# Attention and retention steps placed one piece earlier beside the input projection

## The chip, the cores and the metric

One core of one Trainium2 chip runs the whole kernel. The metric is the device time of the kernel in microseconds (us), the median of several runs.

## The reference

One encoder layer on 256 frames of width 2048, all in float32:

```python
h = rms_norm(x, norm1_g)
proj = h @ w_in                 # 2048 x 7168: retention q,k,v,gate and attention q,k,v
ret = silu(rg) * head_group_norm(retention(rotary(rq), rotary(rk), rv))        # 8 heads of 128
att = chunk_attention(rms_norm(aq), rms_norm(ak), av, rel_bias)                # 8 heads of 128
x = x + concatenate([ret, att]) @ w_out
x = x + square(relu(rms_norm(x) @ w_ff1)) @ w_ff2                              # width 8192
```

Retention multiplies the scores of a head with a decay mask that is causal over chunks of 64 frames; attention is a softmax over the scores plus a bias.

## The kernel before

**Products in three passes.** Each float32 matrix is split into a high part and a rest. For every piece of weights ScalarE writes the high part (`w_hi`, `in_hi`, L993), VectorE subtracts it from the raw weights (`w_lo`, `in_lo`, L1403), and TensorE runs three passes: high by high (L739), low input by high weight (L746), high input by low weight (L752). The last pass alone needs `w_lo`.

**The input stage.** The projection is done in four blocks of two heads each (i = 0 to 3; attention heads 2i and 2i + 1, retention heads u = 2i and 2i + 1). A block walks through 19 slabs, each of two pieces, so 38 pieces with positions 0 to 37:

```python
STEPS = "I0 I1 I2 I3 J0 Q1 J1 P5 J2 P6 J3 P7 P3 Z1 Q2 Z2 P4 H1 H2".split()
```

I and J are the two attention heads (384 columns); the others are the retention columns of both heads (512 columns), where seven products (Q1, P5, P6, P7, P3, Q2, P4) stand for eight, after Strassen and Winograd. So the first half of Q1 is position 10, J1 is 12 and 13, P5 is 14 and 15, P6 is 18 and 19, J3 20 and 21, P7 22 and 23, Z1 26 and 27, P4 32 and 33, H1 34 and 35, H2 36 and 37. P5 and P6 need sums of raw slabs, made by VectorE (`in_sum`, L1412); P7 and P4 need a further slab that a GpSimd DMA adds. `set_y` and `set_h` (ScalarE) and `set_z` and `set_w` (VectorE) move the common products between banks; the second tile of Z1 waits for `set_w`. For block 0 alone VectorE also builds the combinations of the input (`s_first`, L1431, four additions; `s_second`, `s_third`, `s_lo`), and ScalarE their high parts (`s_hi`).

**Attention and retention run beside it.** Each step of a head is a function on one engine: TensorE transposes q and k (`att_T`), ScalarE and VectorE scale them (`att_qT`, `att_kT`), TensorE makes the scores, VectorE adds the bias and takes the maximum, ScalarE takes the exponential, VectorE normalises (`att_probs`), TensorE transposes (`att_PT`) and multiplies with v (`att_pv`), and `att_mix` on ScalarE and then on VectorE splits the result. Ahead of them `att_squares` (ScalarE), `att_mean_squares` (VectorE, writes `a_ms`), a power on GpSimd (`a_rs`, L534) and `att_norm` (VectorE, writes `a_qk`) normalise q and k. Retention is alike: `ret_proj` (ScalarE), `ret_rotate` and `ret_rotated` (VectorE, the latter writes `r_qk`), `ret_T`, `ret_qT`, `ret_kT`, `ret_scores`, `ret_decay`, `ret_y`, `ret_norm`, a power on GpSimd (`r_rs`, L538), `ret_scale`, `ret_ZT`, `ret_mix`.

**What sets the order.** Nothing is scheduled at run time. Each engine has a list written by hand: `at_piece(i, pos, f, h)` puts step f at piece pos of block i. The loops are

```python
for q in range(8 * G_OUT):        # TensorE
    in_piece(q)
    for f in work.get(q, ()): f()
for q in range(8 * G_OUT):        # ScalarE with in_hi, VectorE with in_lo
    in_hi(q + 2)
    for f in work.get(q, ()): f()
```

so TensorE runs a step right after its piece, and ScalarE and VectorE run it after the split of the piece two further on. Steps of one position run in the order in which they were listed. An engine works strictly in its order and waits on semaphores, so a step that is late holds up all that stands behind it. `in_hi(q)` waits until piece q - 4 is used up. The loads of raw slabs (SyncE's queue) wait for `in_lo` of the slab that had the buffer.

After the input stage the output projection (from `G_OUT` on) and the two feed-forward products run; the change doesn't touch them.

Of the kernel before, what the change touches and what calls it, by code (L numbers as in the profile page):

```python
# [39 lines left out]
PIECES = 8  # L40
# [34 lines left out]
def hybrid_block(nc, x, x_cols, w_att, w_ret, w_out, w_up, w_down, gains, rel_windows, rope_cos, rope_sin, decay, out):  # L75
# [3 lines left out]
    with ExitStack() as ctx:  # L79
# [501 lines left out]
        def _(pe):  # L581
# [185 lines left out]
            def at_piece(i, pos, f, *args):  # L767
                work.setdefault(IN_PIECES * i + pos, []).append(lambda: f(*args))

            for i in range(BLOCKS):  # L770
                for h, places in ((2 * i, (13, 15, 19, 21)), (2 * i + 1, (27, 28, 31, 33))):
                    for pos, f in zip(places, (att_T, att_scores, att_PT, att_pv)):
                        at_piece(i, pos, f, h)
                at_piece(i, 35, ret_T, 2 * i)
                at_piece(i, 36, ret_scores, 2 * i)
                at_piece(i, 37, ret_y, 2 * i)
                at_piece(i + 1, 1, ret_ZT, 2 * i)
# [187 lines left out]
        def _(act):  # L965
# [174 lines left out]
            for f, pos in enumerate((9, 10, 13, 14)):  # L1140
                at_piece(0, pos, s_hi, f)
            for i in range(BLOCKS):
# [4 lines left out]
                at_piece(i, 13, att_qT, h)  # L1147
                at_piece(i, 16, keep_in_p5, i)
                at_piece(i, 17, att_exp, h)
                at_piece(i, 19, att_pT, h)  # L1150
                at_piece(i, 21, att_mix, h)
                at_piece(i, 22, att_proj, h + 1)
                at_piece(i, 23, set_y, i)
                at_piece(i, 24, att_squares, h + 1)
                at_piece(i, 25, set_h, i)
                at_piece(i, 27, att_qT, h + 1)
                at_piece(i, 29, att_exp, h + 1)
                at_piece(i, 31, att_pT, h + 1)
                at_piece(i, 32, ret_proj, u)
                at_piece(i, 33, att_mix, h + 1)  # L1160
                at_piece(i, 34, ret_exp, u)
                at_piece(i, 35, ret_qT, u)
                at_piece(i + 1, 0, ret_scale, u)
                at_piece(i + 1, 0, ret_proj, u + 1)
                at_piece(i + 1, 1, ret_mix, u)
# [231 lines left out]
        def _(dve):  # L1397
# [225 lines left out]
            at_piece(0, PIECES - 1, s_first)  # L1623
            at_piece(0, 8, s_second)
            at_piece(0, 10, s_lo, 0)
            at_piece(0, 12, s_third)
            at_piece(0, 13, s_lo, 1)
            at_piece(0, 16, s_lo, 2)
            at_piece(0, 17, s_lo, 3)
            for i in range(BLOCKS):  # L1630
                h, u, late = 2 * i, 2 * i, i == BLOCKS - 1
                at_piece(i, 10, att_mean_squares, h)
                at_piece(i, 11, att_norm, h)
                at_piece(i, 11, in_sum, i, "b", "Q1")
                at_piece(i, 13, att_kT, h)
# [327 lines left out]
```

## Time and profile before

| | |
|---|---|
| median of 3 runs | 1124.0 us (1123.88 to 1124.03) |
| the profiled execution | 1123.88 us, its span 1122.1 us |
| TensorE matmul busy | 1104.2 us, 98% of the span |
| VectorE busy | 884.6 us, 79% |
| ScalarE busy | 688.3 us, 61% |
| GpSimd busy | 54.2 us, 5% |
| mean granted TensorE clock | 0.998 of full speed |

The profile is of one execution; its span runs from the first to the last instruction, and 1.78 us of its time lie around the span. Busy time is what an engine spent in instructions. The trace also tells for each idle stretch which instruction of another engine ended it. A block of the input stage takes 86.4 us (Z1 of block 0 starts at 67.07 us, that of block 1 at 153.47 us).

### The profile page before, as it was taken

Reading aid. Unit: us, or ns where it says so; the run is one execution under the profiler, and the core shown is the slowest. Engines: PE = TensorE matmul, PEld = TensorE weight load, DVE = VectorE, ACT = ScalarE, POOL = GpSimd, SP = SyncE. Lnnn points to the kernel's source line nnn. Section 1 sums busy time; section 2 is a strip of 40 time slices with the busy share of each in tenths; the row PEclk is TensorE's granted clock in tenths of the full one; section 3 lists DMA queues with packets and bytes.
Section 4 is the critical chain, followed back from the end, with each engine's and each line's share of the span. In section 5 each row is a group of like instructions: output and inputs, shape, how many; then the busy total and the mean of one; then the engine's idle time right before and its main releaser. Section 6 shows DMA issues by size and latency. Waiting matters only on the chain.

```text
span 1122.1 us, 13185 instructions
## 1 busy us (share of the span) xinstructions
PE 1104.2 (98%) x5198; PEld 933.7 (83%) x5198; DVE 884.6 (79%) x881; ACT 688.3 (61%) x809; POOL 54.2 (5%) x66
## 2 busy tenths in 40 slices
PE   9799999999999999999999999999999999999998
PEld 9688888988988888888888888888888888888887
DVE  6878777777787768878788778788779788779784
ACT  6565565574565446668756568655667755577652
POOL 0100100100100000000000000000000000000000
PEclk9999999999999999999999999999999999999999
DMA  9785584585576556796797797797787797787792
GB/s 363 261 248 182 156 271 161 166 264 174 169 241 262 187 225 188 230 294 218 233 284 241 249 275 228 230 292 230 262 263 229 247 273 236 257 280 218 246 276 95
DMA packets 42958, 263.81 MB, mean 235 GB/s; under 512 B 4752, under 2 KB 6544, under 8 KB 15120
## 3 DMA queue, kind: packets, MB, share of 16 engines
q1 hardware_dynamic: 36704, 220.22, 52.6%
q0 software_dynamic: 5760, 41.95, 20.3%
q8 instruction: 41, 0.67, 0.2%
q10 hardware_dynamic: 432, 0.81, 0.2%
q14 instruction: 21, 0.17, 0.0%
HBM read 260.85 MB, written 2.10 MB: 234 GB/s over the span
## 4 chain that ended last, share of the span: by engine, by line
PE 85%; DVE 7%; ACT 3%; issue 2%; POOL 1%; ACTq 0%; DVEq 0%
PE acc L869 10%; PE acc L867 10%; PE acc L871 10%; PE acc L739 5%; PE acc L746 5%; PE acc L752 5%; PE bankC L829 4%; PE bankC L824 4%; PE acc L824 4%; PE acc L822 4%; PE bankC L822 4%; PE acc L829 4%; DVE w_lo L1403 3%; PE acc L591 2%; PE acc L596 2%
## 5 line engine op out<-in xcount | busy, mean ns | idle before, releaser
L1690 DVE TENSOR_TENSOR w_lo<-raw,w_hi 128x2048 fp32r<-128x2048 f32 x180 | 410.9, 2288 | 126.9 <-ACT w_hi L1206 126.7
L1206 ACT ACTIVATE w_hi<-raw 128x2048 fp32r<-128x2048 f32 x180 | 344.7, 1916 | 219.5 <-PE acc L871 145.5
L1403 DVE TENSOR_TENSOR w_lo<-raw,w_hi 128x1024 fp32r<-128x1024 f32 (+1 forms) x152 | 167.5, 1106 | 52.4 <-ACT w_hi L993 52.3
L993 ACT ACTIVATE w_hi<-raw 128x1024 fp32r<-128x1024 f32 (+1 forms) x152 | 143.1, 963 | 40.9 <-DVE raw L1412 32.5
L739 PE MATMUL acc<-w_hi,hT_hi 128*128 128x384 f32 (+1 forms) x416 | 105.5, 372 | 0.3 <-ACT w_hi L993 0.2
L867 PE MATMUL acc<-w_hi,hF_hi 128*128 128x512 f32 x256 | 100.8, 394 | 0.0
L871 PE MATMUL acc<-w_hi,hF_lo 128*128 128x512 f32 x256 | 99.7, 390 | 0.0
L869 PE MATMUL acc<-w_lo,hF_hi 128*128 128x512 f32 x256 | 99.7, 389 | 0.0
L746 PE MATMUL acc<-w_hi,hT_lo 128*128 128x384 f32 (+1 forms) x416 | 99.2, 356 | 0.0
L752 PE MATMUL acc<-w_lo,hT_hi 128*128 128x384 f32 (+1 forms) x416 | 98.9, 356 | 0.0
L867 PE MATMUL acc<-w_hi,dF_hi 128*128 128x512 f32 x248 | 96.9, 391 | 0.0
L871 PE MATMUL acc<-w_hi,dF_lo 128*128 128x512 f32 x248 | 96.5, 389 | 0.0
L869 PE MATMUL acc<-w_lo,dF_hi 128*128 128x512 f32 x248 | 96.5, 389 | 0.0
L746 PEld LDWEIGHTS acc<-w_hi,hT_lo 128*128 128x128 f32 x416 | 75.6, 188 | 7.0
L752 PEld LDWEIGHTS acc<-w_lo,hT_hi 128*128 128x128 f32 x416 | 75.4, 188 | 6.5
L739 PEld LDWEIGHTS acc<-w_hi,hT_hi 128*128 128x128 f32 x416 | 72.8, 188 | 6.5 <-ACT w_hi L993 1.0
L1698 DVE TENSOR_TENSOR raw<-raw 128x2048 f32<-128x2048 f32 x32 | 73.1, 2285 | 0.0
L871 PEld LDWEIGHTS acc<-w_hi,hF_lo 128*128 128x128 f32 x256 | 48.0, 188 | 10.1
L867 PEld LDWEIGHTS acc<-w_hi,hF_hi 128*128 128x128 f32 x256 | 48.1, 188 | 9.9
L869 PEld LDWEIGHTS acc<-w_lo,hF_hi 128*128 128x128 f32 x256 | 48.1, 188 | 9.4
L871 PEld LDWEIGHTS acc<-w_hi,dF_lo 128*128 128x128 f32 x248 | 46.6, 188 | 9.7
L867 PEld LDWEIGHTS acc<-w_hi,dF_hi 128*128 128x128 f32 x248 | 46.6, 188 | 9.6
(262 smaller groups left out, 1813.8 us busy)
## 6 DMA issues: line engine op xcount, KB each, us to landing
raw<-in_w_up SPq DMA_DIRECT2D x64, 1024.0 KB, 6.2
raw<-in_w_down SPq DMA_DIRECT2D x64, 1024.0 KB, 6.1
raw<-in_w_ret SPq DMA_DIRECT2D x32, 1024.0 KB, 5.3
raw<-in_w_att SPq DMA_DIRECT2D x28, 768.0 KB, 4.2
raw<-in_w_out SPq DMA_DIRECT2D x16, 1024.0 KB, 4.9
raw<-in_w_up POOLq DMA_DIRECT2D x16, 1024.0 KB, 8.9
raw<-in_w_down POOLq DMA_DIRECT2D x16, 1024.0 KB, 8.6
raw<-in_w_ret POOLq DMA_DIRECT2D x8, 1024.0 KB, 8.5
```

The costliest lines, as they stand in the source:

```text
L739: nc.tensor.matmul(bank[:, 0:wide], stationary(step, m, t)[0], piece(w_hi, q, start, start + wide), start=fresh, stop=False, skip_group_ch ...
L746: nc.tensor.matmul(bank[:, 0:n], stationary(step, m, t)[1], piece(w_hi, q, start, start + n), start=False, stop=False, skip_group_check=True)
L752: mm = nc.tensor.matmul(bank[:, 0:n], stationary(step, m, t)[0], piece(w_lo, q, start, start + n), start=False, stop=t == SLAB_KT - 1, ski ...
L822: nc.tensor.matmul(bank[:], hi[:, form, tile_cols(t)], wh[:, cols], start=first and t == 0, stop=False, skip_group_check=True)
L824: nc.tensor.matmul(bank[:], lo[:, form, tile_cols(t)], wh[:, cols], start=False, stop=False, skip_group_check=True)
L867: nc.tensor.matmul(banks[m][:], hi[:, form + m, tile_cols(t)], wh[:, cols], start=False, stop=False, skip_group_check=True)
L869: nc.tensor.matmul(banks[m][:], hi[:, form + m, tile_cols(t)], wl[:, cols], start=False, stop=False, skip_group_check=True)
L871: mm = nc.tensor.matmul(banks[m][:], lo[:, form + m, tile_cols(t)], wh[:, cols], start=False, stop=t == SLAB_KT - 1, skip_group_check=True)
L993: nc.scalar.activation(piece(w_hi, q, 0, n), raw[:, r, half * n:(half + 1) * n], ACT.Copy).then_inc(hi_done, 1)
L1206: nc.scalar.activation(w_hi[:, ring(s)], raw[:, r, :], ACT.Copy).then_inc(slab_hi, 1)
L1403: nc.vector.tensor_tensor(piece(w_lo, q, 0, n), raw[:, IN_PLAN[i, READ_AT.get(step, step)][0], half * n:(half + 1) * n], piece(w_hi, q, 0, ...
L1690: nc.vector.tensor_tensor(w_lo[:, ring(s)], raw[:, r, :], w_hi[:, ring(s)].bitcast(f32), ALU.subtract).then_inc(slab_lo, 1)
```

## The change

Only positions in the three lists change; no instruction is added or removed. Most steps of attention and the retention steps of the first head of a block move one piece earlier on all three engines. Some go otherwise: on VectorE `s_first` moves from position 7 to 8 and `s_third` from 12 to 9; `in_sum` of P5 moves ahead of `in_lo` of the piece 13 and of `att_norm`; `ret_rotate` stays at 33 and `ret_rotated` at 34; `set_w` goes from 23 to 24 and the second head's `att_mean_squares` stays at 24, now behind it. On ScalarE the second head's `att_squares` and `set_y` change places. GpSimd's and SyncE's programs are the same.

```diff
@@ TensorE
-                for h, places in ((2 * i, (13, 15, 19, 21)), (2 * i + 1, (27, 28, 31, 33))):
-                    for pos, f in zip(places, (att_T, att_scores, att_PT, att_pv)):
-                        at_piece(i, pos, f, h)
-                at_piece(i, 35, ret_T, 2 * i)
-                at_piece(i, 36, ret_scores, 2 * i)
-                at_piece(i, 37, ret_y, 2 * i)
-                at_piece(i + 1, 1, ret_ZT, 2 * i)
+                for h, first in ((2 * i, 12), (2 * i + 1, 26)):
+                    at_piece(i, first, att_T, h)
+                    at_piece(i, (14, 27)[h % 2], att_scores, h)
+                    at_piece(i, (18, 30)[h % 2], att_PT, h)
+                    at_piece(i, (20, 32)[h % 2], att_pv, h)
+                at_piece(i, 34, ret_T, 2 * i)
+                at_piece(i, 35, ret_scores, 2 * i)
+                at_piece(i, 36, ret_y, 2 * i)
+                at_piece(i + 1, 0, ret_ZT, 2 * i)
@@ ScalarE
-            for f, pos in enumerate((9, 10, 13, 14)):
+            for f, pos in enumerate((9, 10, 12, 13)):
                 at_piece(0, pos, s_hi, f)
...
-                at_piece(i, 13, att_qT, h)
+                at_piece(i, 12, att_qT, h)
                 at_piece(i, 16, keep_in_p5, i)
-                at_piece(i, 17, att_exp, h)
-                at_piece(i, 19, att_pT, h)
-                at_piece(i, 21, att_mix, h)
+                at_piece(i, 16, att_exp, h)
+                at_piece(i, 18, att_pT, h)
+                at_piece(i, 20, att_mix, h)
                 at_piece(i, 22, att_proj, h + 1)
-                at_piece(i, 23, set_y, i)
-                at_piece(i, 24, att_squares, h + 1)
+                at_piece(i, 23, att_squares, h + 1)
+                at_piece(i, 24, set_y, i)
                 at_piece(i, 25, set_h, i)
-                at_piece(i, 27, att_qT, h + 1)
-                at_piece(i, 29, att_exp, h + 1)
-                at_piece(i, 31, att_pT, h + 1)
+                at_piece(i, 26, att_qT, h + 1)
+                at_piece(i, 28, att_exp, h + 1)
+                at_piece(i, 30, att_pT, h + 1)
                 at_piece(i, 32, ret_proj, u)
-                at_piece(i, 33, att_mix, h + 1)
-                at_piece(i, 34, ret_exp, u)
-                at_piece(i, 35, ret_qT, u)
-                at_piece(i + 1, 0, ret_scale, u)
+                at_piece(i, 32, att_mix, h + 1)
+                at_piece(i, 33, ret_exp, u)
+                at_piece(i, 34, ret_qT, u)
+                at_piece(i, 37, ret_scale, u)
                 at_piece(i + 1, 0, ret_proj, u + 1)
-                at_piece(i + 1, 1, ret_mix, u)
+                at_piece(i + 1, 0, ret_mix, u)
@@ VectorE
-            at_piece(0, PIECES - 1, s_first)
+            at_piece(0, 8, s_first)
             at_piece(0, 8, s_second)
+            at_piece(0, 9, s_third)
             at_piece(0, 10, s_lo, 0)
-            at_piece(0, 12, s_third)
-            at_piece(0, 13, s_lo, 1)
-            at_piece(0, 16, s_lo, 2)
-            at_piece(0, 17, s_lo, 3)
+            at_piece(0, 11, s_lo, 1)
+            at_piece(0, 13, s_lo, 2)
+            at_piece(0, 15, s_lo, 3)
...
                 at_piece(i, 10, att_mean_squares, h)
+                at_piece(i, 10, in_sum, i, "b", "Q1")
                 at_piece(i, 11, att_norm, h)
-                at_piece(i, 11, in_sum, i, "b", "Q1")
-                at_piece(i, 13, att_kT, h)
+                at_piece(i, 12, att_kT, h)
                 at_piece(i, 14, in_sum, i, "d", "P5")
-                at_piece(i, 15, att_bias_max, h)
-                at_piece(i, 18, att_probs, h)
+                at_piece(i, 14, att_bias_max, h)
+                at_piece(i, 17, att_probs, h)
                 at_piece(i, 20, set_z, i)
-                at_piece(i, 21, att_mix, h)
-                at_piece(i, 23, set_w, i)
+                at_piece(i, 20, att_mix, h)
+                at_piece(i, 24, set_w, i)
                 at_piece(i, 24, att_mean_squares, h + 1)
-                at_piece(i, 26, att_norm, h + 1)
-                at_piece(i, 27, att_kT, h + 1)
-                at_piece(i, 28, att_bias_max, h + 1)
-                at_piece(i, 30, att_probs, h + 1)
+                at_piece(i, 25, att_norm, h + 1)
+                at_piece(i, 26, att_kT, h + 1)
+                at_piece(i, 27, att_bias_max, h + 1)
+                at_piece(i, 29, att_probs, h + 1)
+                at_piece(i, 32, att_mix, h + 1)
                 at_piece(i, 33, ret_rotate, u)
-                at_piece(i, 33, att_mix, h + 1)
                 at_piece(i, 34, ret_rotated, u)
-                at_piece(i, 35, ret_kT, u)
+                at_piece(i, 34, ret_kT, u)
                 at_piece(i, 35, ret_sigmoid, u)
-                at_piece(i, 36, ret_decay, u)
-                at_piece(i, 37, ret_norm, u)
+                at_piece(i, 35, ret_decay, u)
+                at_piece(i, 36, ret_norm, u)
...
-                at_piece(i + 1, 1, ret_mix, u)
+                at_piece(i + 1, 0, ret_mix, u)
```

## Rows read from the trace of the kernel before

**Rows 1.** The page, engines: busy us, share of the span, instructions.

```profile
PE 1104.2 (98%) x5198; PEld 933.7 (83%) x5198; DVE 884.6 (79%) x881; ACT 688.3 (61%) x809; POOL 54.2 (5%) x66
```

**Rows 2.** Windows: one block, all after the input stage; stretch, length, busy, clock, DMA.

```profile
104.00:190.00 86.00, 83.86 (x434) 73.93 (x433) 66.77 (x113) 49.09 (x91) 5.86 (x6) 1.00 0.63 200
440.00:1122.00 682.00, 679.26 (x3076) 564.03 (x3075) 546.20 (x344) 436.46 (x374) 27.51 (x32) 1.00 0.78 245
```

**Rows 3.** What TensorE waited for, 20 to 366 us: total us, times, longest.

```profile
PE bankD L739 <- ACT w_hi L993: 4.4, 4, 2.6
PE bankB L639 <- DVE a_p L1512: 3.0, 4, 1.4
PE bankC L752 <- DVE w_lo L1403: 2.9, 6, 0.8
PE bankA L652 <- DVE r_qk L1538: 2.6, 4, 0.9
```

**Rows 4.** Timeline of block 0: start us, us, instruction, in brackets idle before.

```profile
26.83 2.50 DVE L1431 TENSOR_TENSOR s_blk<-hT_hi,hT_lo 128x512 f32<-128x512 f32 x4
27.71 1.06 ACT L993 ACTIVATE w_hi<-raw 128x1024 fp32r<-128x1024 f32 x1 [1.75 <-DMA raw<-in_w_ret]
...
33.11 0.73 PE L752 MATMUL bankC<-w_lo,hT_hi 128*128 128x512 f32 x2 [0.79 <-DVE w_lo L1403]
...
41.48 1.22 PE L739 MATMUL bankD<-w_hi,sf_hi 128*128 128x512 f32 x2 [2.63 <-ACT w_hi L993]
...
56.39 0.55 PE L639 MATMUL bankB<-ident,a_p 128*128 128x128 f32 x3 [1.40 <-DVE a_p L1512]
```

**Rows 5.** Windows: the stretch just after block 0's longest wait.

```profile
41.50:44.80 3.30, 3.30 (x8) 2.63 (x9) 3.30 (x4) 2.78 (x5) 0.21 (x1) 0.50 0.74 117
```

**Rows 6.** Timeline of block 1, positions 11 to 19.

```profile
124.52 0.95 DVE L1403 TENSOR_TENSOR w_lo<-raw,w_hi 128x768 fp32r<-128x768 f32 x1
124.69 1.64 POOL L534 TENSOR_TENSOR a_rs<-a_ms,neg_half 128x4 f32<-128x4 f32 x1 [8.60 <-DVE a_ms L1479]
...
127.16 2.29 DVE L1412 TENSOR_TENSOR raw<-raw 128x2048 f32<-128x2048 f32 x1
...
129.40 0.38 PE L624 MATMUL bankA<-ident,a_qk 128*128 128x128 f32 x2
...
142.79 0.55 PE L639 MATMUL bankB<-ident,a_p 128*128 128x128 f32 x3 [0.53 <-DVE a_p L1512]
```

**Rows 7.** Timeline of GpSimd's powers, 20 to 160 us.

```profile
27.07 1.02 POOL L527 TENSOR_TENSOR rstd<-me,neg_half 128x2 f32<-128x2 f32 x1 [25.57 <-DVE me L1614]
...
115.39 0.70 POOL L538 TENSOR_TENSOR r_rs<-r_ve,neg_half 128x2 f32<-128x2 f32 x1 [14.72 <-DVE r_ve L1569]
...
154.57 1.03 POOL L534 TENSOR_TENSOR a_rs<-a_ms,neg_half 128x4 f32<-128x4 f32 x1 [12.20 <-DVE a_ms L1479]
```

**Rows 8.** Timeline of block 1, `set_y` and `set_w`.

```profile
151.29 0.61 ACT L1089 ACTIVATE acc<-bankC 128x512 f32<-128x512 f32 x1
...
152.59 0.69 DVE L1425 TENSOR_TENSOR acc<-in_p,bankC 128x512 f32<-128x512 f32 x1
```

**Rows 9.** Timeline of block 1, from the end of `att_pv` to `ret_T`.

```profile
171.74 0.38 PE L645 MATMUL bankA<-a_pT,a_proj 128*128 128x128 f32 x2
...
172.18 0.39 ACT L1045 ACTIVATE zT_hi<-bankA 128x256 fp32r<-128x256 f32 x1
172.32 1.22 DVE L1403 TENSOR_TENSOR w_lo<-raw,w_hi 128x1024 fp32r<-128x1024 f32 x1 [0.87 <-ACT w_hi L993]
...
174.94 0.42 DVE L1517 TENSOR_TENSOR zT_lo<-bankA,zT_hi 128x256 fp32r<-128x256 f32 x1
...
176.41 0.69 DVE L1538 TENSOR_TENSOR r_qk<-r_c,r_s 128x512 f32<-128x512 f32 x1
...
177.44 0.38 PE L652 MATMUL bankC<-ident,r_qk 128*128 128x128 f32 x2
```

**Rows 10.** Timeline of block 1, `ret_T` of the second head of block 0.

```profile
107.73 0.44 PE L652 MATMUL bankA<-ident,r_qk 128*128 128x128 f32 x2 [0.58 <-DVE r_qk L1538]
```

## The prediction

> **What bounds the kernel now.** I read the page first: TensorE is busy for 98% of the span [rows 1]. The windows by stage say where the rest is: 682 us after the input stage hold under 3 us of idle TensorE, while one block of the input stage holds 2.1 us in 86 us [rows 2]. So the change can only act on TensorE's waits in the four blocks. The waits of that stretch sum to 12.9 us in 18 waits [rows 3]: four of `ret_T` for `r_qk`, which belong to the second heads, and the others around P5, P6 and `att_PT`. The timeline then shows the order of events. Block 0 has the worst: 0.79 us in Q1, 2.63 us before P5, 1.40 us before `att_PT` [rows 4]. After the 2.63 us of idleness the granted clock is 0.50, the level of 1.2 GHz, for 3.4 us [rows 5], and P5 pays about 1.7 us; after 1.40 us it stays at 1.00. The stage is balanced so finely that a position moved by one piece (1.4 us for half of P4, P5 or P6, 2.1 us for J, 2.7 us for Z and H) matters only by what waits for it.
>
> I follow the new lists by hand with the old durations. A split of 1024 columns takes 1.06 us on ScalarE [rows 4] and 1.22 us on VectorE [rows 9], and the next instruction begins 0.08 us before the end; one of 768 takes 0.95 us on VectorE and gives way after 0.87 [rows 6].
>
> **Block 0, its head.** `s_first` (2.50 us [rows 4]) ran while VectorE had to wait anyway: piece 10's high part ends at 28.77 because its load is late [rows 4]. At position 8 it runs behind `in_lo` of piece 10, so VectorE idles 1.9 us and then does 28.79 + 1.14 + 2.53 (`s_first`) + 1.33 (`s_second`) = 33.79 before `in_lo` of piece 11. Q1's last pass starts at about 35.05 in place of 33.11 [rows 4]. From there VectorE itself is the chain, with everything ahead of `att_PT` on it: splits, `s_third` 1.20, two `in_sum` of 2.20, three `s_lo` of 0.60, `att_norm` 0.79, `att_kT` 0.40, `att_bias_max` 1.38, `att_probs` 0.74, and one wait of 0.7 for piece 15. It sums to `a_p` at 55.05, against 56.33. `att_T` in the meantime waits until 42.3 and TensorE is idle 3 to 4 us. `att_PT` starts 1.3 us sooner, but one half of P6 (1.37 us) now stands behind it: the head of block 0 comes out at 0.0 us, up to +0.4 if P5 and J1 run at the low clock again.
>
> **Blocks 1 to 3, their head.** `in_sum` (2.29 us) may start where piece 13's split started, at 124.52, in place of 127.16 [rows 6]. That makes P5's high part early, and pushes `in_lo` of 13 and `att_norm` behind it: 124.52 + 2.20 + 0.87 + 0.11 (for `a_rs`, below) + 0.87 = 128.57. TensorE ends the first half of J1 at 127.32 and wants `att_T` there; it ran at 129.40 before [rows 6]. New wait 1.3 us, where the waits in P5 (1.2 us with the restarts) go. On along VectorE: splits of 14 to 19, `in_sum`, `att_kT`, `att_bias_max` and `att_probs`, with 0.8 us of waiting for high parts, give `a_p` at 140.34, against 142.7 before; `att_PT` starts 2.4 us earlier than 142.79 [rows 6], less 1.37 for the half of P6 that is now behind it: gain 1.0 us in each of three blocks, 3.0 in all. Bounds: 0 if the order on VectorE stretches by another 1.0, and 1.5 if `a_p` is ready when TensorE asks.
>
> **Z1, every block.** Counted from the start of P7, `set_y` ran at 3.38 and `set_w` at 4.68 (P7 at 147.91) [rows 8]. With `att_squares` (1.17) ahead of it on ScalarE, `set_y` goes to 4.7 at its end and `set_w` to 6.17 at its end, behind `in_lo` of piece 26. Z1's second tile asks at 5.95: 0.27 us and a restart, 0.35 (bounds 0 and 0.6). Then `att_mean_squares` comes at 6.1 with `in_lo` of 27 right behind it. GpSimd's power `a_rs` takes 1.03 us beside an idle VectorE [rows 7] and 1.64 us when it starts inside a split [rows 6], ending 0.86 us after that split's end. So it ends at 7.37 + 0.86 = 8.23, `a_qk` at 9.14, and `att_T`, wanted at 8.58, waits 0.62 and a restart: 0.70 (bounds 0, if `a_rs` takes 1.03, and 1.0). Sum 1.05 us, four times 4.2.
>
> The case that most divides these sums is that power. The rows say: 1.64 within a split; and a power of two columns takes 1.02 us, begun amid four additions back to back, against 0.70 us alone [rows 7], so it gets in when one instruction ends and need not wait for the last. That gives the 0.11 us above. The Trainium skill, page "SBUF — State Buffer", section "Who interferes with whom", has the rule: a VectorE instruction with two inputs in SBUF and a GpSimd instruction that reads SBUF share one read port, and the second blocks until the first ends. By that rule, the trace agrees; a power that overlaps freely would take 1.03 everywhere and the total below would be 2.8 lower.
>
> **`ret_T` of the first head, every block.** This is the largest term. `ret_T` moves from behind H1's second half to behind its first, 2.72 us. What feeds it is moved less. `att_pv` ends at 172.12; ScalarE then splits `zT_hi`, then the high part of a piece, and VectorE from the low part of that piece (172.32) to the end of `r_qk` (177.10) needs 4.78 us, 0.34 of it the rest of `att_mix` [rows 9]. Now `in_hi` of piece 35 stands behind `att_mix`, and VectorE's `in_lo` of 35 behind that, with `ret_rotate` and `ret_rotated` still at 33 and 34. From the end of `att_pv`: 0.06 + 0.26 + 1.06 + 0.02 + 4.44 = 5.84 us. TensorE, from the same point, has the second half of P4 (1.46) and the first of H1 (2.72), less 0.24 by which the next piece overlaps the end: 3.94. Before, both halves of H1 lay there and 0.3 us was to spare [rows 9]. So TensorE waits 1.9 us, with restart 2.0, and four times 8.0. Each duration is a row's, and both sides hang on TensorE's own `att_pv`, so I hold it to 1.7 to 2.2 a block. The steps behind it (`ret_decay`, `ret_norm`, `ret_scale`, `ret_ZT`) have over 0.5 us to spare each; loads and the GpSimd DMAs are asked for no later relative to their use.
>
> **`ret_T` of the second head.** It waited 0.58 us, with restart and pipeline end 0.83 [rows 10], three times, and 1.2 in the last block (0.9 in [rows 3]). `ret_ZT` and `ret_mix` of the first head now run one piece earlier, and `r_qk` comes 1 us before it is asked for. Gain 3.7 us; below, 0.
>
> **Sum.** 0.0 - 3.0 + 4.2 + 8.0 - 3.7 = +5.5 us, against the profiled execution's own 1123.88: 1129.4; that execution lies 0.1 under the median, so 1129.4 stands for either. Outside the input stage nothing moves.
>
> **The rivals.** (B) GpSimd isn't held and `set_w` is in time: 4.2 falls away, +1.3, 1125.3, no measurable change. The two lengths of `a_rs` speak against it, the small slack of `set_w` for it. 22%. (C) Faster: ScalarE and VectorE reach `r_qk` before the new `ret_T`. It decides at 1.9 us less than the 5.84 of that chain, and would take the 8.0 away: -2.5, 1121.4. Also here: the early moves bring what the waits before P5, P6 and `att_PT` suggest. [Rows 9] speak against it. 11%. (D) GpSimd is kept out until VectorE truly idles: in the head the power then ends one split later, 1.0 us a block, +4.0, 1133.3. The 1.02 us row speaks against it. 8%. (E) The clock falls to the 1.2 GHz level after each new `ret_T` wait, as it did after 2.63 us, and takes 1.7 us each: +6.8, 1136.1. The idle time there is some 1.7 us by the profile's count, nearer the 1.40 that left the clock alone. 7%. The Trainium skill, page "TensorE: Matmul & The Clock Gate", section "HAM oscillation — how this bites in real kernels", tells that a wait that recurs in a loop can bring the low clock back each time; by it the time would be E's. The forecast has 52%, its own range 1127.0 to 1131.5.
>
> **How the numbers follow.** The range takes in B and most of D: 1123.8 to 1133.0; C and E are left out. About 0.2% (2.2 us) is what a measurement tells from no change. Slower by more: forecast, D and E, less 3% for a small forecast, 0.64. The same: B and that edge, 0.25. Faster: C, 0.11.
>
> **What would show it.** Right: `ret_T` on banks C and D waits for `r_qk` some 1.7 us four times, and no longer on bank A; `att_T` waits for `a_qk` over 1 us; the wait of L739 on bank D is gone; `a_rs` takes some 3 us at the heads. Wrong: no wait at `ret_T` of the first heads (C), a clock of 0.50 after them (E), `a_rs` of 1.03 in the second heads (B), or block 0's head more than 1 us off.

## The result, and the profile after

The changed kernel takes 1133.4 us (median of four runs, 1133.2 to 1134.0); beside it the kernel before took 1123.9 us (1123.8 to 1124.0). The ratio is 1.0085, 95% interval 1.0067 to 1.0102: slower by 9.4 us. The forecast was 1129.4 with a range up to 1133.0, so the direction was right and the size was not. The profiled execution of the changed kernel took 1134.24 us, 10.36 more than that of before. One of the six runs of experiment 11 took 6357 us and is left out of the range given there.

The page of the changed kernel, engines:

```profile
PE 1105.7 (98%) x5198; PEld 935.2 (83%) x5198; DVE 887.1 (78%) x881; ACT 690.2 (61%) x809; POOL 64.3 (6%) x66
```

Against [rows 1] TensorE, VectorE and ScalarE do the same work in 1.5 to 2.5 us more; GpSimd alone is busy 10 us longer, with the same 66 instructions. The page's view says nothing more: 10 us of lost time hide behind a rounded 98%.

One block, from Z1 to the next Z1, and work after the input stage, by windows (stretch, length, then busy time of TensorE's matmuls and weight loads, VectorE, ScalarE and GpSimd, granted clock, DMA):

```profile
69.60:157.80 88.20, 84.45 (x435) 74.36 (x434) 67.75 (x113) 49.97 (x91) 8.05 (x6) 1.00 0.62 195
337.00:1120.00 783.00, 780.74 (x3542) 647.50 (x3541) 626.11 (x453) 494.15 (x449) 29.95 (x36) 1.00 0.76 242
```

The second stretch has 2.3 us of idle TensorE in 783, as little as in [rows 2]; the block has grown from 86.4 to 88.2 us, and 3.75 us of it are idle against 2.1. So the loss is in the input stage, where the changed lists are.

What TensorE waited for in the changed kernel (total us, times, longest):

```profile
PE bankA L624 <- DVE a_qk L1488: 9.0, 8, 3.9
PE bankC L652 <- DVE r_qk L1540: 7.2, 4, 1.8
PE bankC L752 <- DVE w_lo L1405: 3.2, 1, 3.2
...
PE acc L739 <- DVE acc L1427: 0.8, 4, 0.2
```

(Line numbers of ScalarE and VectorE are two higher than before; two waits of 1.6 us, which lie before 20 us, are left out.) The waits of P5 for `w_hi`, of `att_PT` for `a_p` and of the second head's `ret_T` on bank A [rows 3] are gone. In their place stand eight of `att_T`, four of the first heads' `ret_T` on bank C, four for `set_w`, and one of 3.2 us in block 0. The change exchanged waits, and the new ones are longer.

**Block 0** is the first place to look. Its timeline (start, length, instruction, in brackets the idle time before it and what ended it):

```profile
35.33 1.22 PE L752 MATMUL bankC<-w_lo,hT_hi 128*128 128x512 f32 x2 [3.17 <-DVE w_lo L1405]
...
43.53 0.69 PE L624 MATMUL bankA<-ident,a_qk 128*128 128x128 f32 x2 [3.85 <-DVE a_qk L1488]
```

and what VectorE and GpSimd did ahead of the second wait, from their timelines:

```profile
37.94 2.28 DVE L1414 TENSOR_TENSOR raw<-raw 128x2048 f32<-128x2048 f32 x1
40.14 0.95 DVE L1405 TENSOR_TENSOR w_lo<-raw,w_hi 128x768 fp32r<-128x768 f32 x1
41.01 0.68 DVE L1451 TENSOR_TENSOR sf_lo<-s_mix,sf_hi 128x512 fp32r<-128x512 f32 x1
42.60 0.87 DVE L1488 TENSOR_SCALAR a_qk<-a_proj,a_rs 128x128 f32<-128x128 f32 x4 [0.91 <-POOL a_rs L534]
```

```profile
38.11 4.46 POOL L534 TENSOR_TENSOR a_rs<-a_ms,neg_half 128x4 f32<-128x4 f32 x1 [2.74 <-DVE a_ms L1481]
```

The power on four columns took 4.46 us. It began in `in_sum`, lasted through the split and `s_lo`, and ended at 42.57, 0.88 after the last of the three. `att_norm` stood behind it, and VectorE was idle 0.91 us. What became of that at `att_PT`, with one more wait of VectorE on the way:

```profile
46.13 1.23 DVE L1405 TENSOR_TENSOR w_lo<-raw,w_hi 128x1024 fp32r<-128x1024 f32 x1 [0.97 <-ACT w_hi L995]
...
56.46 0.35 DVE L1514 TENSOR_SCALAR a_p<-a_e,a_rc 128x256 f32<-128x256 f32 x1
...
57.58 0.49 PE L639 MATMUL bankB<-ident,a_p 128*128 128x128 f32 x3
```

`a_p` ends at 56.81, and TensorE asks for it at 57.58. The clock is in the windows:

```profile
35.00:39.00 4.00, 3.67 (x12) 3.41 (x13) 4.00 (x7) 2.29 (x6) 1.26 (x2) 0.57 1.05 387
39.00:43.00 4.00, 0.67 (x4) 0.35 (x3) 3.09 (x6) 2.06 (x3) 4.00 (x2) 0.89 0.27 77
43.00:50.00 7.00, 6.47 (x23) 6.17 (x24) 5.96 (x9) 3.52 (x5) 0.58 (x1) 0.58 1.00 221
50.00:54.00 4.00, 4.00 (x23) 3.69 (x22) 3.93 (x9) 2.85 (x7) 0.00 (x0) 1.00 0.09 18
```

The clock fell to the 1.2 GHz level with each of the two waits; before it fell once [rows 5]. A mean of 0.57 over 4 us is 0.50 for 3.4 us; the next two rows give another 0.9 and 5.9 us in the same way, 10.2 us in all against 3.3 in [rows 5]. Against the same pieces of block 1, the end of Q1 and the first half of J1 took 1.6 us more, and `att_T` with the second half of J1 and the first half of P5 2.5 us more. The first 1.6 us cost nothing: TensorE was done at 39.68 and then stood still for 3.85 us until `a_qk` came. The starts of the pieces give the balance: J3 begins 2.61 us later than before. The two waits are 7.0 us; before there were five, of 0.62, 0.79, 2.63, 0.37 and 1.40, together 5.8 us, each with its restart (the first products after a wait take longer: `att_T`'s two took 0.44 us in block 1 of the changed kernel and 0.38 in that of before). In the last row TensorE is busy without a gap, and it stays so through P6: `a_p` is ready when P6's half ends.

**Blocks 1 to 3, their heads.** The piece starts show J3 0.84 us earlier against Q1 in each block, and 0.89 up to Z1 (forecast 1.0). The timeline of block 1 has the power of 2.98 us that the prediction worked out, and the wait of `att_T` that it said:

```profile
129.96 2.98 POOL L534 TENSOR_TENSOR a_rs<-a_ms,neg_half 128x4 f32<-128x4 f32 x1 [8.61 <-DVE a_ms L1481]
...
133.92 0.44 PE L624 MATMUL bankA<-ident,a_qk 128*128 128x128 f32 x2 [1.18 <-DVE a_qk L1488]
```

**Z1 to H1** costs 1.54 us a block (forecast 1.05). Block 1's timeline, TensorE and GpSimd:

```profile
158.67 0.73 PE L739 MATMUL acc<-w_hi,hT_hi 128*128 128x512 f32 x2 [0.21 <-DVE acc L1427]
158.77 1.93 POOL L534 TENSOR_TENSOR a_rs<-a_ms,neg_half 128x4 f32<-128x4 f32 x1 [12.58 <-DVE a_ms L1481]
...
161.67 0.44 PE L624 MATMUL bankA<-ident,a_qk 128*128 128x128 f32 x2 [0.41 <-DVE a_qk L1488]
...
170.86 0.35 DVE L1514 TENSOR_SCALAR a_p<-a_e,a_rc 128x256 f32<-128x256 f32 x1
...
171.26 0.55 PE L639 MATMUL bankB<-ident,a_p 128*128 128x128 f32 x3
```

The wait for `set_w` with its restart costs about 0.45 us and that of `att_T` about 0.55. The last two rows are one that no list of waits names: `a_p` ends at 171.21 and `att_PT` begins at 171.26. Before, `a_p` ended 0.7 us ahead of it. The transpose is not shown as waiting since the modelled end of the piece ahead covers the gap, but the piece starts grow by 0.4 us there.

**`ret_T` of the first heads.** Both sides, as worked out, in block 1 (VectorE's chain, then TensorE):

```profile
177.01 0.42 DVE L1519 TENSOR_TENSOR zT_lo<-bankA,zT_hi 128x256 fp32r<-128x256 f32 x1 [1.33 <-ACT zT_hi L1047]
177.96 1.23 DVE L1405 TENSOR_TENSOR w_lo<-raw,w_hi 128x1024 fp32r<-128x1024 f32 x1 [0.52 <-ACT w_hi L995]
...
180.58 1.22 DVE L1405 TENSOR_TENSOR w_lo<-raw,w_hi 128x1024 fp32r<-128x1024 f32 x1
181.72 0.68 DVE L1540 TENSOR_TENSOR r_qk<-r_c,r_s 128x512 f32<-128x512 f32 x1
```

```profile
182.46 0.44 PE L652 MATMUL bankC<-ident,r_qk 128*128 128x128 f32 x2 [1.79 <-DVE r_qk L1540]
```

VectorE is idle 1.33 us until `att_pv` and ScalarE's split are done, 0.52 more for the next high part, and only then come `ret_rotate`, a split and `ret_rotated`. It is idle with work in hand: the rotation needs nothing of `att_pv`.

### The profile page after: what moved, and what is told of

Same layout as the page of the kernel before. It is cut to its first block, busy times and chain, and to the rows that moved or that the text cites. A ratio compares the mean times of both kernels' runs of the same rounds, so it can differ in the third digit from the quotient of the medians.

```text
span 1132.4 us, 13184 instructions
## 1 busy us (share of the span) xinstructions
PE 1105.7 (98%) x5198; PEld 935.2 (83%) x5198; DVE 887.1 (78%) x881; ACT 690.2 (61%) x809; POOL 64.3 (6%) x66
## 4 chain that ended last, share of the span: by engine, by line
PE 82%; DVE 6%; ACT 5%; issue 3%; POOL 2%; DMA 2%; ACTq 0%; DVEq 0%
PE acc L873 10%; PE acc L871 10%; PE acc L869 10%; PE bankC L831 4%; PE acc L831 4%; PE bankC L826 4%; PE acc L826 4%; PE acc L824 4%; PE bankC L824 4%; PE acc L739 4%; PE acc L746 4%; PE acc L752 4%; ACT w_hi L995 3%; DVE w_lo L1405 2%; PE acc L591 2%
## 5 line engine op out<-in xcount | busy, mean ns | idle before, releaser
L739 PEld LDWEIGHTS acc<-w_hi,hT_hi 128*128 128x128 f32 x416 | 73.4, 191 | 10.2 <-DVE acc L1427 2.5
```

The source lines that it names most:

```text
L739: nc.tensor.matmul(bank[:, 0:wide], stationary(step, m, t)[0], piece(w_hi, q, start, start + wide), start=fresh, stop=False, skip_group_ch ...
```

## The experiments

Times are medians; the kernel before ran beside each set, at 1123.91, 1123.96, 1124.05 and 1124.08 us. Where a block is named, differences come from the starts of its pieces.

### 1. The changed kernel once more

> The changed kernel as it is. If the longer time of block 0's head comes from the order of the lists, GpSimd's first power a_rs is again 4.4 to 4.5 us long, the clock is again low for about 10 us in all around 36 to 49 us, and the time is 1133.4 within 0.7. If it came from chance (the phase of a clock window or a late load in that one execution), the first power or the low stretches differ and the time moves by up to 2 us.

1133.7 us (1133.4 to 1133.9), ratio 1.0086 (1.0071 to 1.0101). Every power of the input stage came back at the same length, 4.46 us too, and every wait but one, so they follow from the lists. The one is `att_T`'s in block 0, 3.15 us in place of 3.85, and the clock has changed beside it:

```profile
39.00:43.00 4.00, 1.29 (x5) 0.78 (x3) 3.09 (x6) 2.06 (x3) 4.00 (x2) 0.50 0.26 61
...
46.00:50.00 4.00, 4.00 (x18) 3.73 (x17) 3.96 (x4) 2.11 (x4) 0.00 (x0) 0.73 0.97 199
```

These are windows of its block 0. Here the clock stays low from the wait in Q1 on, through the idle time ahead of `att_T`, where the other execution had it back for a while, and it rises about 0.8 us sooner behind. TensorE takes longer for J1 and waits that much less: `att_T` starts at 43.43 against 43.53. Behind it `att_PT` starts at 57.16 against 57.58, and J3 is 2.2 us late in place of 2.6. So the low clock in the head is no accident of one execution, but its borders move; ahead of `att_T` it costs nothing, behind `att_T` it does.

### 2. `s_first` back at position 7

```diff
-            at_piece(0, 8, s_first)
+            at_piece(0, PIECES - 1, s_first)
```

> The changed kernel with s_first back at position 7, in VectorE's idle time. Theory (VectorE's order sets block 0's head): Q1's last pass comes 2 us earlier, att_T about 2.2 us earlier, and the head and the whole kernel gain about 2.0 us, 1131.4. Rival (GpSimd's held power or the low clock sets it alone): att_T moves by less than 0.5 us or the low clock takes the gain back, and the kernel stays at 1133.4 within 0.5.

1131.4 us (1131.3 to 1131.6), ratio 1.0066 (1.0049 to 1.0083): 2.4 us back against experiment 1, the changed kernel in the same set. The wait in Q1 is 0.8 us again, and the low clock behind it is gone; behind `att_T` it is low for one stretch of 3.4 us, as long as before. The waits:

```profile
PE bankA L624 <- DVE a_qk L1488: 10.3, 8, 5.1
...
PE bankC L752 <- DVE w_lo L1405: 1.4, 2, 0.8
```

All of block 0's loss goes (J3 at -0.3 against before), although `att_T` now waits 5.1 us and the power is still 4.46 us long. So the four additions in the wrong gap are what this kernel loses in block 0. Their way there is VectorE's own chain: `a_qk` begins 2.1 us sooner (40.48 against 42.60) and `a_p` ends 2.1 to 2.2 us sooner (54.59 against 56.71 in experiment 1 and 56.81). That leaves at most 0.3 us of the 2.5 at J3 against experiment 1 for the clock.

### 3. `s_lo(1)` of block 0 behind `att_norm`

```diff
-            at_piece(0, 11, s_lo, 1)
...
                 at_piece(i, 11, att_norm, h)
+                if i == 0:
+                    at_piece(0, 11, s_lo, 1)
```

> The changed kernel with one VectorE step of block 0, s_lo of the second combination, moved from ahead of att_norm to behind it. Theory (GpSimd's power is held while VectorE goes from one instruction with two inputs in SBUF straight to the next, and got in early in blocks 1 to 3 because att_norm had to wait there): the first a_rs falls from 4.46 us to 2.98 as in the other blocks, or to 3.8 if it has to let the split of piece 13 pass, and att_T of block 0 starts 0.9 to 1.5 us earlier. The kernel gains 0.5 to 1.5 us, for the low clock takes part of it. Rival (something else of block 0 holds the power, such as the DMA traffic of the first 40 us): it stays at 4.46 and att_T where it was.

1132.9 us (1132.7 to 1133.3), ratio 1.0080 (1.0066 to 1.0093), 0.8 less than the changed kernel run again. The first power is shorter by the 0.60 us of the instruction that no longer stands between:

```profile
38.23 3.86 POOL L534 TENSOR_TENSOR a_rs<-a_ms,neg_half 128x4 f32<-128x4 f32 x1 [2.76 <-DVE a_ms L1481]
...
128.35 2.98 POOL L534 TENSOR_TENSOR a_rs<-a_ms,neg_half 128x4 f32<-128x4 f32 x1 [8.61 <-DVE a_ms L1481]
```

In block 0 it ends 0.88 us after piece 13's split, in block 1 0.87 us after the end of `in_sum`, one instruction sooner, and the order on VectorE is the same in both: `in_sum`, split, `att_norm`. So VectorE's back-to-back instructions hold the power in block 0, and something that differs between the blocks decides whether it gets in after one of them. These runs don't show what. `att_T` starts 0.4 to 0.5 us sooner (43.05), less than the 0.9 expected. And the clock is not the same: it is low from 34.3 to 41.1 us and back at 1.00 when `att_T` starts. TensorE then comes to `att_PT` first and waits 1.07 us for `a_p`, which ends at 55.88, and J3 is 1.0 us late. So with the clock up it is VectorE's chain that sets block 0's head, and the 0.8 us hold some of the clock.

### 4. `ret_rotate` ahead of `att_mix`, one position earlier

```diff
+                at_piece(i, 32, ret_rotate, u)
                 at_piece(i, 32, att_mix, h + 1)
-                at_piece(i, 33, ret_rotate, u)
-                at_piece(i, 34, ret_rotated, u)
+                at_piece(i, 33, ret_rotated, u)
```

> The changed kernel with ret_rotate of the first head at 32, ahead of att_mix on VectorE, and ret_rotated at 33, behind one split less. Theory (ret_T waits for what VectorE does behind att_mix): the rotation falls into VectorE's wait for att_mix, r_qk comes 1.5 to 2 us earlier, the four waits of ret_T on bank C of 1.8 us go, and the kernel gains 7.5 to 8.0 us: 1125.6. Rival (the wait is only passed on to ret_scores or ret_y, whose chain is also tight): it gains under 3 us, and new waits stand at ret_scores, ret_y or ret_ZT.

1125.8 us (1125.4 to 1126.4, ten runs), ratio 1.0017 (1.0008 to 1.0026): 7.9 us back, the whole term. The waits are those of the changed kernel (the longest of `att_T` 3.8 in place of 3.9) without the row of L652:

```profile
PE bankA L624 <- DVE a_qk L1488: 9.0, 8, 3.8
PE bankC L752 <- DVE w_lo L1405: 3.2, 1, 3.2
```

### 5. The second head's mean squares ahead of `set_w`

```diff
-                at_piece(i, 24, set_w, i)
                 at_piece(i, 24, att_mean_squares, h + 1)
+                at_piece(i, 24, set_w, i)
```

> The changed kernel with the second head's att_mean_squares ahead of set_w, so that GpSimd's power starts beside set_w, which has one input in PSUM, and not inside a split with two inputs in SBUF. Theory (two SBUF inputs hold GpSimd's read): the four powers of 1.93 us become 1.03, a_qk comes 0.9 us earlier, att_T's wait of 0.41 goes, gain 0.5 to 0.7 us in each block, 2.0 to 2.8 in all: 1131.0. Rival (any VectorE instruction beside it slows the power): it stays at 1.7 or more and the time at 1133.4 within 0.7.

1132.0 us (1130.9 to 1132.1), ratio 1.0069 (1.0054 to 1.0084): 1.7 us back, less than expected: `set_w` itself is now a little later, and the loss at `att_PT` stays. The mechanism shows in block 1's timeline:

```profile
157.46 0.69 DVE L1427 TENSOR_TENSOR acc<-in_p,bankC 128x512 f32<-128x512 f32 x1
...
157.64 1.03 POOL L534 TENSOR_TENSOR a_rs<-a_ms,neg_half 128x4 f32<-128x4 f32 x1 [11.98 <-DVE a_ms L1481]
158.06 1.22 DVE L1405 TENSOR_TENSOR w_lo<-raw,w_hi 128x1024 fp32r<-128x1024 f32 x1
...
158.20 0.74 PE L739 MATMUL acc<-w_hi,hT_hi 128*128 128x512 f32 x2 [0.28 <-DVE acc L1427]
```

Begun beside `set_w`, which reads one operand from PSUM, the power takes 1.03 us, as begun beside an idle VectorE [rows 7], and a split that starts later doesn't hold it. The second heads' `att_T` no longer waits. Rival B's price for the power (1.03 us) is thus what another order gives; in the changed kernel it was 1.93 us.

### 6. All three together

> The three edits to the changed kernel at once: s_first at 7, ret_rotate ahead of att_mix at 32 with ret_rotated at 33, att_mean_squares ahead of set_w. Theory (they take away separate waits): the gains add, 2.2 + 7.8 + 1.7 = 11.7 us off 1133.5, so 1121.8, which is faster than before. Rival (they cover each other, or a wait removed late in a block returns in the next head): 1124 or more.

1121.5 us (1121.2 to 1122.3, eleven runs), ratio 0.9979 (0.9970 to 0.9987). The three parts add up: 2.4 + 7.9 + 1.7 is 12.0, and 12.2 came back. With them the changed lists are faster than those before, by 2.4 us.

The head of block 0 has the same order on every engine as in experiment 2, and its profiled execution prices the clock. `att_T` starts at 41.41 in experiment 2 and at 41.47 here; behind it the clock is low for 3.4 us there and for 6.1 here. `att_PT`, first there and then here:

```profile
54.65 0.55 PE L639 MATMUL bankB<-ident,a_p 128*128 128x128 f32 x3
```

```profile
55.85 0.49 PE L639 MATMUL bankB<-ident,a_p 128*128 128x128 f32 x3
```

That is 1.2 us for one longer low stretch, and 1.2 at J3 too (-0.3 and +0.9). `a_p` itself ends at 54.59 and 55.03, so up to 0.4 us of it comes through VectorE's chain. The eleven runs spread over 1.1 us.

### 7. The first head's `att_T` at 13 again

```diff
-                for h, first in ((2 * i, 12), (2 * i + 1, 26)):
+                for h, first in ((2 * i, 13), (2 * i + 1, 26)):
...
-                at_piece(i, 12, att_qT, h)
+                at_piece(i, 13, att_qT, h)
...
-                at_piece(i, 12, att_kT, h)
+                at_piece(i, 13, att_kT, h)
```

> The changed kernel with the first head's att_T, att_qT and att_kT back at position 13 and all else as changed. Theory (att_T at 12 asks 1.3 us too early and stops TensorE, while att_PT is set by VectorE's order): the wait of 1.2 us goes in all blocks, block 0 idles 2.5 us in place of 3.9, and blocks 1 to 3 gain about 0.7 us each at J3; in all 2.1 to 4 us: 1130.5. Rival (the early att_T pays for itself by an earlier a_p): no gain or a loss, 1133.5 to 1135.

1130.4 us (1130.2 to 1130.5), ratio 1.0057 (1.0041 to 1.0072), 3.4 us better than the changed kernel run again, as expected. TensorE does half of J1 in place of waiting:

```profile
PE bankB L639 <- DVE a_p L1514: 2.6, 4, 0.9
PE bankA L624 <- DVE a_qk L1488: 2.2, 5, 0.6
```

`att_PT` waits instead, 0.9 us at most, and `att_scores` of block 0 once, 1.3 us, but that costs less than the 1.2 to 3.9 us at the first heads' `att_T`. About half of the gain, 1.6 us at J3, is block 0's, where the clock is also low for 6.8 us in place of 13.7.

### 8. The kernel before with the retention part alone

```diff
-                at_piece(i, 35, ret_T, 2 * i)
-                at_piece(i, 36, ret_scores, 2 * i)
+                at_piece(i, 34, ret_T, 2 * i)
+                at_piece(i, 35, ret_scores, 2 * i)
...
-                at_piece(i, 34, ret_exp, u)
+                at_piece(i, 33, ret_exp, u)
```

and likewise `ret_y`, `ret_ZT`, `ret_qT`, `ret_kT`, `ret_decay`, `ret_norm`, `ret_scale` and `ret_mix`; `ret_rotate` and `ret_rotated` stay.

> The kernel before with the retention part of the change alone: ret_T, ret_scores, ret_y, ret_ZT of the first head and what belongs to them on ScalarE and VectorE one piece earlier, attention untouched. Theory (ret_T of the first head cannot be moved without its rotation): r_qk ends at 177.1 as before while TensorE asks at 174.7, a wait of 2.4 us and restart, four times 2.5 lost, 3.7 gained at the second head's ret_T: +6.3, 1130.2. Rival (the loss comes only together with att_pv's move, since the rotation hangs on it): under 2 us lost, 1126 or less.

1132.2 us (1131.8 to 1132.4), ratio 1.0072 (1.0058 to 1.0086): 8.2 us slower than before, where 6.3 was expected. Blocks 0 and 2 lose 1.75 us each on balance, and block 1 3.4. The timeline and a window there say why:

```profile
178.70 0.66 PE L652 MATMUL bankC<-ident,r_qk 128*128 128x128 f32 x2 [2.28 <-DVE r_qk L1538]
...
179.44 2.06 PE L739 MATMUL acc<-w_hi,hT_hi 128*128 128x512 f32 x4
```

```profile
179.10:182.50 3.40, 3.40 (x12) 2.77 (x11) 1.74 (x3) 2.06 (x3) 0.00 (x0) 0.55 0.02 5
```

The four products of the pass take 2.06 us where they take 1.17 at full clock: the 1.2 GHz level after one wait of 2.28 us. The other three waits of that length left the clock at 1.00. This is the event of rival E, once in four and worth 1.65 us. Where the wait is 1.79 us, as in the changed kernel, it never came: 24 waits in the six profiled executions that have it.

### 9. The same with `ret_rotate` at 32 and `ret_rotated` at 33

> The kernel before with the retention part of the change, and ret_rotate at 32 and ret_rotated at 33. Theory (the rotation's place is the whole cause of the loss with the retention part): no wait at the first heads' ret_T, none at the second heads', so 3.5 us under the kernel before: 1120.4. Rival (ret_T at 34 passes its wait on to a later step): 1123 or more.

1121.2 us (1120.9 to 1121.6, eight runs), ratio 0.9975 (0.9965 to 0.9985). The rotation stands ahead of `att_mix`. The waits of the input stage are those of [rows 3] with the same numbers, less the last row, that of `ret_T`, and with one of 0.2 us more. So the second head's gain is real, and all but a little of the first head's cost was in the rotation's place. By the piece starts the second heads give the 3.7 us of the changed kernel, and the first heads still cost 0.3 us a block, which they don't in experiment 6 (`ret_T` of block 1 begins 0.06 us after the end of `r_qk` here, at 174.12, and 0.73 after it there); that is why 2.8 us came of the 3.5 expected.

### 10. `att_norm` ahead of `in_sum`

All three edits of experiment 6, and

```diff
-                at_piece(i, 10, att_mean_squares, h)
+                at_piece(i, 9, att_mean_squares, h)
+                at_piece(i, 10, att_norm, h)
                 at_piece(i, 10, in_sum, i, "b", "Q1")
-                at_piece(i, 11, att_norm, h)
```

with `s_third` at 11 and the third `s_lo` at 15 in block 0.

> The kernel with all three edits, and its head ordered anew on VectorE: att_mean_squares of the first head at 9, where VectorE has 0.7 us free, att_norm at 10 ahead of in_sum, s_third at 11 and the third s_lo at 15. Theory (the power inside in_sum and the norm behind it made att_T at 12 wait): the power is 1.03 to 1.1 us long in blocks 1 to 3, att_T's wait of 1.2 us goes, but att_PT stays bound by VectorE's order, so only 0.4 us a block are gained there; block 0 gains 1.5. In all 1121.5 - 2.7 = 1118.8. Rival (att_T's wait was harmless and what sets the head is only the sum of VectorE's work): 1121 to 1122.

1119.7 us (1119.6 to 1120.0), ratio 0.9962 (0.9950 to 0.9974), 1.8 us better than experiment 6 and 0.9 worse than expected. The first heads' powers take 1.01 to 1.07 us, the clock stays at 1.00 throughout the input stage, but `att_PT` waits 3.2 us in its four places. Blocks 1 to 3 gain 0.4 us each, as expected. Block 0's J3 is at -0.3 against before, no sooner than in experiment 2 with the power held for 4.46 us; so its gain here is against the low clock of experiment 6, and a free power has brought nothing there beside a changed order.

### 11. The three edits and `att_T` at 13

> The kernel with all three edits, and att_T, att_qT, att_kT of the first head back at 13. Theory (the gain of 3.1 us that this gave on the changed kernel does not depend on the other edits): 1121.5 - 3 = 1118.5. Rival (in block 0 it shared its gain with s_first): block 0 gives under 1 us, and the kernel 1120.

1117.8 us (1117.7 to 1117.8), ratio 0.9944 (0.9931 to 0.9957), the fastest kernel here: 6.2 us below the kernel before, and 0.7 better than expected. Block 0 gains 1.2 us at J3 against experiment 2, so the rival falls.

### 12. Experiments 10 and 11 together

> The three corrections (s_first back at 7, ret_rotate at 32, the second head's mean squares ahead of set_w) with both further moves together: the first head's att_T, att_qT and att_kT at 13, and att_mean_squares at 9, att_norm at 10 ahead of in_sum. With att_T at 13 alone the time was 1117.8, and waits of att_T for a_qk were only 1.4 us in all there; what stays are att_PT's waits for a_p, about 0.6 us in each block. My theory: VectorE's own sum sets a_p, and the power no longer does, so taking the power out of in_sum (1.07 in place of 2.98 us) is worth 0.2 us a block at most and 0.5 to 1 us in block 0: 1117.0 (1116.3 to 1117.8). Rival: the power's hold still delays att_norm and all of VectorE's chain behind it to a_p, since VectorE stands in att_norm while it waits; then 1 us a block falls away, and the time is 1114 to 1115.

1119.7 us (1119.4 to 1120.1), ratio 0.9962 (0.9948 to 0.9975). Neither side had this: 1.9 us slower than experiment 11. First experiment 11 in block 1 (VectorE, then TensorE), then this one:

```profile
123.10 2.29 DVE L1414 TENSOR_TENSOR raw<-raw 128x2048 f32<-128x2048 f32 x1
...
126.29 0.90 DVE L1488 TENSOR_SCALAR a_qk<-a_proj,a_rs 128x128 f32<-128x128 f32 x4
...
127.98 0.38 PE L624 MATMUL bankA<-ident,a_qk 128*128 128x128 f32 x2
```

```profile
123.80 0.87 DVE L1488 TENSOR_SCALAR a_qk<-a_proj,a_rs 128x128 f32<-128x128 f32 x4
124.59 2.28 DVE L1414 TENSOR_TENSOR raw<-raw 128x2048 f32<-128x2048 f32 x1
...
129.43 1.23 DVE L1405 TENSOR_TENSOR w_lo<-raw,w_hi 128x1024 fp32r<-128x1024 f32 x1 [0.20 <-ACT w_hi L995]
130.57 0.48 DVE L1494 TENSOR_SCALAR a_kT<-bankB,gv 128x256 f32<-128x256 f32 x1
...
131.19 0.46 PE L632 MATMUL bankA<-a_kT,a_qT 128*128 128x128 f32 x2 [0.45 <-DVE a_kT L1494]
```

In experiment 11 `a_qk` is ready 0.8 us before `att_T` wants it, with the power held for 2.98 us: the hold runs beneath `in_sum` and a split that VectorE had to do anyway. Here `a_qk` is 4 us early, and `in_sum` comes 0.7 us later relative to the pieces; P5's high parts wait for it, VectorE waits for them, and `att_scores` waits 0.45 us for `a_kT`. By the piece starts blocks 1 to 3 lose 0.3 us each that way. The other 0.8 us are block 0's: J1's second half waits 2.71 us for `w_lo` in place of 1.28 and `att_T`, which waited 1.42, doesn't, so that P5 starts as before, but `att_PT` gets `a_p` 0.8 us later. Freeing the power bought nothing, and its price was paid beside it.

## Why the prediction was wrong in size

On the profiled executions, each term of the sum beside what the piece starts give:

| term | forecast | measured |
|---|---|---|
| block 0, its head | 0.0 (to +0.4) | +2.6 |
| blocks 1 to 3, their head | -3.0 | -2.7 |
| Z1, every block | +4.2 | +6.2 |
| `ret_T` of the first head | +8.0 | +8.0 |
| `ret_T` of the second head | -3.7 | -3.7 |
| sum | +5.5 | +10.4 |

**The step that failed is the head of block 0**, put at 0.0 and measured at +2.6. The order of events was right: VectorE became the chain, and Q1's last pass was forecast at 35.05 and came at 35.33. What was mis-sized is that chain: `a_p` was forecast at 55.05 and ended at 56.81, 1.8 us late, and `att_PT` can't start before it. The largest part is the power. It was given 0.11 us beyond `in_sum`'s split in blocks 1 to 3 and nothing of its own in block 0; there it was held through three instructions, as rival D said of it, VectorE stood idle 0.91 us, and `att_T`, forecast at 42.3, came at 43.53. The wait for piece 15's high part was 0.97 us in place of 0.7, the chain began 0.26 us later than forecast, and the rest, 0.3 us, is in small gaps. (The prediction names three `s_lo`; its sum holds four, and four ran.)

The second part is the clock. TensorE, at the low level until 48.9, asks for `a_p` at 57.58, 0.8 us after its end; in experiment 1 it is 0.4 us. The prediction had this as "up to +0.4 if P5 and J1 run at the low clock again". But its own forecast held an idle stretch of 2.7 us in Q1 (the old 0.79 and 1.94 more) and one of 3 to 4 before `att_T`, both longer than the 2.63 us after which [rows 5] show 1.2 GHz, and both were followed by it; so some price belonged in the sum. Some of the lateness of `a_p` may be the clock's too, up to 0.4 us by experiments 2 and 6. The exact shares stay open: with another order of the head (experiment 10) a free power brought block 0 nothing, so what it would bring in this order isn't shown. What is shown is that moving `s_first` alone takes the whole loss away (experiment 2), and that with the clock up behind `att_T` VectorE's chain still sets `att_PT` (experiment 3).

**Z1** is a mis-sized term, by 0.5 us a block, 2.0 in all, the second largest part of the miss. The wait for `set_w` (0.35 forecast, some 0.45) and that of `att_T` (0.70, some 0.55, and experiment 5 recovers about as much) were near. The third, 0.4 us at the second heads' `att_PT`, had not been looked for: the prediction followed the chain to `att_T` and stopped, while `a_p` had only 0.7 us to spare. (Its wait of `att_T`, 0.62 us, is 0.56 by its own 9.14 and 8.58.)

**`ret_T` of the first head** and **of the second** were right by mechanism and size: an idle time of 1.79 us four times, and the whole 8 us back in experiment 4. **Blocks 1 to 3** were right within 0.3 us; the power of 2.98 us and the wait of 1.18 against 1.3 are as worked out.

**The rivals.** B fell: `a_rs` took 1.93 us at the second heads and `set_w` was late. C fell as the lists stand; experiments 4 and 9 show that the place of `ret_rotate` alone made `r_qk` late. D holds in block 0 and not in the others, so neither it nor the forecast's rule (the power gets in when one instruction ends) holds everywhere. E did not come in the changed kernel, and came once in four in experiment 8. The Trainium skill, page "TensorE: Matmul & The Clock Gate", section "HAM oscillation — how this bites in real kernels", tells that a wait recurring in a loop brings the low clock back each time; its case has waits of some 3 to 5 us. These traces agree for the waits of 3.2 and 3.9 us in block 0, and not for the shorter recurring ones of 1.79 us (never) and 2.28 us (one in four). The Trainium skill, page "SBUF — State Buffer", section "Who interferes with whom", says that a VectorE instruction with at most one input in SBUF, outside the modes that use two ports, leaves GpSimd alone, and one with two holds a GpSimd instruction that reads SBUF; experiment 5 agrees on both sides, 1.03 us begun beside `set_w` and 1.93 beside a split. The VectorE instructions in a row that held it were one, two or three here.

What stays open is why the power of block 0 is held by one instruction more than those of blocks 1 to 3 with the same order on VectorE. Experiment 3 took one instruction out of the hold and gave 0.8 us, in part by the clock.

## What to carry to other kernels

Before pulling a consumer forward on the bounding engine, pull its producers forward on theirs, and look first for one that stands in a list behind work it doesn't need: two lines of `ret_rotate` were worth 7.9 us, where the whole move, with its three faults mended, was worth 2.4. Where an engine is the chain, add up what it will stand and wait for, a result of GpSimd that it holds up itself included, and not only its own instructions. When a forecast itself holds a new idle stretch of TensorE as long as one that the trace shows followed by the low clock, the clock has a price, and the price depends on where TensorE waits next: here nothing ahead of `att_T`, and 0.4 to 0.8 us behind it (1.2 in experiment 6). And a held instruction costs only if its result is wanted in that time: in experiment 11 a power of 2.98 us is free, and in experiment 12 making it 1.0 us, at the expense of what stood behind it, made the kernel slower.

## What the runs showed of the hardware

The same power on four columns took 1.01 to 1.07 us begun while VectorE was idle or in `set_w`, 1.57 to 1.66 begun within a split of 768 columns, 1.93 within one of 1024, 2.98 within `in_sum`, and 3.86 or 4.46 in block 0, and each of the held ones ended 0.86 to 0.89 us after the end of some VectorE instruction. A split that began 0.42 us after the power, behind `set_w`, did not lengthen it (1.03 us). The clock's fall after a wait is not the same each time: four equal waits of 2.28 us in one execution were followed by it once, and in two executions of the changed kernel the same lists left one unbroken low stretch or two. Nor does the length of one wait decide it: in experiment 11 the clock was at 0.50 from 41.9 to 45.1 us, right behind two waits of only 1.28 and 1.42 us that lie 1.0 us apart, while the single wait of 1.40 us in [rows 4] left it at 1.00.
